# Feed-forward and MLP products: four high-weight products in a row, then four low-weight ones, in place of two and two

## Chip, cores and metric

The kernel runs on one core of a Trainium2 chip. The metric is the device time of one execution in microseconds (us). Before the change it is 2199.45 us, the median of three runs (2197.57 to 2200.47).

## What is computed

Two conditioned transformer stacks, one after the other, on 256 tokens of width 1024, all in float32. The first has two layers, each with a SwiGLU feed-forward of inner width 2816, a token mixer with two attention branches, and a second feed-forward. The second stack has a scan mixer, a window attention and three squared-ReLU MLPs of inner width 4096 (one of them for the context tokens). The change touches only the products of these two functions:

```python
def swiglu(x, w_gate, w_up, w_down):
    return (jax.nn.silu(x @ w_gate) * (x @ w_up)) @ w_down

def sq_relu_mlp(h, w1, w2):
    return jnp.square(jax.nn.relu(h @ w1)) @ w2
```

`swiglu` is called four times (stages F0, F1, F2, F3 of the kernel), `sq_relu_mlp` three times (Mc, M0, M1).

## The kernel before

**Float32 in three products.** A float32 matrix product is built from single-pass products of rounded operands (type fp32r). A weight w is split into a high part and a low part, w = hi + lo: ScalarE rounds a loaded chunk into `whi` (L1406), VectorE subtracts to get `wlo` (L1910). Activations are split the same way, and the two parts of one block of 128 features lie beside each other: 256 columns high, then 256 columns low. `xs` holds the split input of a stage (8 blocks), and `hs`, `hidden_arena`, `hidden_nraw` and `hidden_table` hold the split hidden values (22 blocks in a feed-forward, 32 in an MLP).

For one 128x128 block of weights TensorE issues two matmuls. `wide_hi` (L619) takes the high weights as the stationary operand and streams all 512 columns, high and low activations together, into one full bank of PSUM. `wide_lo` (L623) takes the low weights and streams the 256 high columns into the first half of the same bank. Each matmul has a weight load of its own, since no two neighbours use the same weights. In this document a "high step" or "hi" is a matmul of L619 and a "low step" or "lo" one of L623.

**Chunks.** Weights come from memory in chunks of 1 MB (2048 float32 in each of 128 partitions) through a ring of three: SyncE issues the load into `stage`, ScalarE writes `whi`, VectorE writes `wlo` and raises `lo_done`, TensorE uses the chunk and raises `chunk_used` with its last matmul, after which ScalarE may overwrite that `whi`. A chunk of the wide path is 16 weight blocks, so 16 hi and 16 lo.

**Order on TensorE.** It is written out by hand in the tensor block. `wide_first` (the first chunk of a stage) goes hi, hi, lo, lo over two output blocks of one input block, since its inputs arrive one by one. `wide_up` (all other chunks of the first products) takes one output block (`f`) at a time and goes through the eight input blocks `k` in pairs: hi of k and k+1, then lo of k and k+1. `wide_down` (second products) takes one of four output blocks (`d`) at a time and goes through the chunk's hidden blocks in pairs in the same way: four blocks in most chunks, two in the chunk of blocks 20 and 21 of a feed-forward, which is used twice. Every wait (for `lo_done`, for a drained bank, for hidden values) stands ahead of a chunk or between two `d`, never inside a pair. The mixers use another helper, `product` (L613, L614, L615), which issues three matmuls of 256 columns for each weight block, again with one weight load each; its order stays as it is. `keep_warm` (L688) issues matmuls of 512 bf16 columns ahead of some stages.

Of the kernel before, what the change touches and what calls it, by code (L numbers as in the profile page):

```python
# [95 lines left out]
class Signal:  # L96
# [15 lines left out]
    def at(self, key):  # L112
        if self.book["known"]:
            return self.book[self.name, key]
        return 1
# [3 lines left out]
def program(nc, A, out_ap, book):  # L119
    ctx = ExitStack()  # L120
    with ctx:
# [308 lines left out]
        def hidden(name, j):  # L430

            if j < 3:
                return hs[:, 2 * j:2 * j + 2, :, :]
            if name[0] == "F":
                at = (0, 4)[j - 3] if j < 5 else 16 + 4 * (j - 5)
                room = hidden_arena[:, at * 256:at * 256 + 1024]
            elif j < 5:
                room = hidden_nraw[:, (j - 3) * 1024:(j - 2) * 1024]
            elif j == 5:
                room = hidden_table[:]  # L440
            else:
                room = hidden_arena[:, (j - 6) * 1024:(j - 5) * 1024]
            return room.rearrange("p (f a t) -> p f a t", f=2, a=2)
# [154 lines left out]
        def _(pe):  # L598
# [18 lines left out]
            def wide_hi(out, w, pair, s, first_mm):  # L617

                return mm(out, whi[:, s, w:w + P], pair.rearrange("p a t -> p (a t)"), start=first_mm, stop=False, skip_group_check=True)  # L619

            def wide_lo(out, w, pair, s, last_mm):

                return mm(out[:, 0:T], wlo[:, s, w:w + P], pair[:, 0, :], start=False, stop=last_mm, skip_group_check=True)  # L623
# [34 lines left out]
            def wide_up(n, banks):  # L658

                pe.wait_ge(lo_done, START + n + 1)  # L660
                for f in range(2):
                    for k in range(0, 8, 2):
                        for kk in (k, k + 1):
                            wide_hi(banks[:, f, :], kk * 256 + f * P, xs[:, kk, :, :], n % RING, kk == 0)
                        for kk in (k, k + 1):
                            last = wide_lo(banks[:, f, :], kk * 256 + f * P, xs[:, kk, :, :], n % RING, kk == 7)
                last.then_inc(chunk_used, 1)

            def wide_down(n, name, blocks, d_at, banks, width, opens, closes, after=None):

                for d in range(4):
                    at = lambda i: i * width + (d_at + d) * P
                    pair = lambda i: hidden(name, blocks[i] // 2)[:, blocks[i] % 2, :, :]
                    for i in range(0, len(blocks), 2):
                        for ii in (i, i + 1):
                            wide_hi(banks[:, d, :], at(ii), pair(ii), n % RING, opens and ii == 0)
                        for ii in (i, i + 1):
                            last = wide_lo(banks[:, d, :], at(ii), pair(ii), n % RING, closes is not None and ii == len(blocks) - 1)
                    if closes and (d < 3 or width == 1024):
                        last.then_inc(pe_out.sem, pe_out.next(("y", name, closes, d)))  # L680
                    if after is not None:
                        after(d)
                return last
# [50 lines left out]
            def ffn(name):  # L734
                n = first[name]
                for j in range(PAIRS):
                    if j == 0:
                        wide_first(n, R[:, 0:2, :], name)
                    else:
                        pe.wait_ge(dve_out.sem, dve_out.at(("gate", name, j - 1)))  # L740
                        wide_up(n + 2 * j, R[:, 0:2, :])
                    turns(name, 2 * j)
                    if j:
                        pe.wait_ge(dve_out.sem, dve_out.at(("up", name, j - 1)))
                    wide_up(n + 2 * j + 1, R[:, 2:4, :])
                    turns(name, 2 * j + 1)
# [7 lines left out]
                for c in range(5):  # L754
                    pe.wait_ge(lo_done, START + n + c + 1)
                    if c == 0:
                        pe.wait_ge(dve_out.sem, dve_out.at(("gate", name, PAIRS - 1)))
                    pe.wait_ge(dve_out.sem, dve_out.at(("lo", name, 2 * c + 1)))
                    wide_down(n + c, name, range(4 * c, 4 * c + 4), 0, R, 512, c == 0, None, free if c == 0 else None) \
                        .then_inc(chunk_used, 1)  # L760
                    turns(name, 2 * PAIRS + c)
                pe.wait_ge(lo_done, START + n + 6)
                pe.wait_ge(dve_out.sem, dve_out.at(("lo", name, 10)))
                wide_down(n + 5, name, range(20, 22), 0, R, 1024, False, "R")
                pe.wait_ge(mod_taken, max(m for (at, w), m in turn_at.items() if at == name and w < 27) + 1)
                wide_down(n + 5, name, range(20, 22), 4, Y, 1024, True, None).then_inc(chunk_used, 1)
                turns(name, 27)

# [10 lines left out]
            def mlp(name):  # L779
                n = first[name]  # L780
                for j in range(UPS):
                    banks = R[:, 2 * (j % 2):2 * (j % 2) + 2, :]
                    if j == 0:
                        wide_first(n, banks, name)
                    else:
                        if j >= 2:
                            pe.wait_ge(dve_out.sem, dve_out.at(("up", name, j - 2)))
                        wide_up(n + j, banks)
                    turns(name, j)
# [1974 lines left out]
```

## Time and profile before

| | |
|---|---|
| median of 3 runs | 2199.45 us |
| profiled execution, its time | 2199.59 us |
| its span, first to last instruction | 2197.7 us |
| TensorE matmul busy | 2134.2 us, 97% |
| TensorE weight load busy | 1869.7 us, 85% |
| VectorE busy | 1799.1 us, 82% |
| ScalarE busy | 1184.3 us, 54% |
| DMA, mean of the span | 230 GB/s |
| mean granted TensorE clock | 0.992 |

The time lies 1.9 us above the span, for what precedes the first and follows the last instruction. Matmuls overlap in the records: a matmul of 512 columns is shown with about 0.39 us and its successor starts about 0.23 us after it. So for the pace of TensorE the distance from start to start counts and not the length of a record. In what follows a "step" is the time from the start of one matmul to the start of the next.

### The profile page before, as it was taken

To read this page: it belongs to the slowest core of one execution; us is meant where nothing else is said; L and a number is where in the kernel's file an instruction comes from. 1 tells how busy PE (TensorE), PEld (TensorE's weight loads), DVE (VectorE), ACT (ScalarE), POOL (GpSimd) and SP (SyncE) were. 2 spreads that over 40 slices of the span, in tenths; PEclk is the share of its full clock that TensorE was granted. 3 is DMA by queue.
4 is the path that set the end of the run, shared out by engine and by line. 5 is a ranking of instruction groups with operands and counts; after the bars stand their busy time and mean duration, and the time that the engine had idled before them with its cause. 6 is when DMAs were issued, how large, how long until landed. Compare 5 with 4: busy or idle time off the path is not lost.

```text
span 2197.7 us, 33877 instructions
## 1 busy us (share of the span) xinstructions
PE 2134.2 (97%) x14000; PEld 1869.7 (85%) x14000; DVE 1799.1 (82%) x2404; ACT 1184.3 (54%) x1785; POOL 109.5 (5%) x157
## 2 busy tenths in 40 slices
PE   7999999999999999999999999999999999999997
PEld 4888888888888889898889979888888888768886
DVE  4988787788878878877888787888998899788764
ACT  3555557455455445665544455447646744485742
POOL 1000000000000000000000000000000000000000
PEclk9999999999999999999999999999999999999999
DMA  9888666488858877655887727728878877405662
GB/s 332 287 285 315 222 221 209 135 269 286 306 197 278 290 251 258 205 183 189 278 288 254 270 92 234 249 78 291 287 284 271 296 257 258 134 5 167 214 211 77
DMA packets 330881, 506.28 MB, mean 230 GB/s; under 512 B 12375, under 2 KB 239926, under 8 KB 330727
## 3 DMA queue, kind: packets, MB, share of 16 engines
q1 hardware_dynamic: 288503, 341.75, 46.6%
q0 software_dynamic: 41616, 160.44, 20.8%
q8 instruction: 111, 1.82, 0.3%
q10 hardware_dynamic: 608, 1.92, 0.3%
q14 instruction: 43, 0.35, 0.0%
HBM read 503.03 MB, written 1.05 MB: 229 GB/s over the span
## 4 chain that ended last, share of the span: by engine, by line
PE 85%; DVE 9%; DMA 2%; ACT 2%; issue 1%; POOL 0%; DVEq 0%; POOLq 0%
PE banks L619 38%; PE banks L623 19%; PE banks L613 6%; PE banks L615 6%; PE banks L614 6%; DVE wlo L1910 1%; DMA plain_xs<-in_ada_w_dram 1%; PE banks L825 1%; PE banks L887 1%; DMA stage<-in_ffn_wg_dram 1%; DVE nraw L2188 1%; DVE arena L1935 1%; DVE xs L2192 1%; PE banks L720 1%; PE banks L721 1%
## 5 line engine op out<-in xcount | busy, mean ns | idle before, releaser
L1910 DVE TENSOR_TENSOR wlo<-stage,whi 128x1024 fp32r<-128x1024 f32 x644 | 758.2, 1219 | 131.2 <-ACT whi L1406 130.4
L1406 ACT CAST whi<-stage 128x1024 fp32r<-128x1024 f32 x644 | 643.7, 1051 | 335.4 <-PE banks L623 256.9
L619 PE MATMUL banks<-xs,whi 128*128 128x512 f32 x2176 | 687.4, 397 | 13.4 <-DVE xs L2192 9.5
L623 PEld LDWEIGHTS banks<-xs,wlo 128*128 128x128 f32 x2176 | 409.6, 188 | 96.9
L623 PE MATMUL banks<-xs,wlo 128*128 128x256 f32 x2176 | 428.2, 278 | 0.0
L613 PE MATMUL banks<-xs,whi 128*128 128x256 f32 x1216 | 351.8, 289 | 10.2 <-DVE xs L2192 4.8
L619 PEld LDWEIGHTS banks<-xs,whi 128*128 128x128 f32 x2176 | 331.6, 189 | 18.4 <-DVE xs L2192 7.6
L614 PE MATMUL banks<-xs,whi 128*128 128x256 f32 x1216 | 344.4, 283 | 0.0
L615 PE MATMUL banks<-xs,wlo 128*128 128x256 f32 x1216 | 344.4, 283 | 0.0
L619 PE MATMUL banks<-hidden_arena,whi 128*128 128x512 f32 x992 | 311.9, 395 | 0.0
L1935 DVE SCALAR_TENSOR_TENSOR arena<-modw,cact,arena 128x1024 f32<-128x1024 f32 x203 | 259.9, 1280 | 8.8 <-DMA modw<-in_w_mod_dram 4.3
L613 PEld LDWEIGHTS banks<-xs,whi 128*128 128x128 f32 x1216 | 233.5, 192 | 20.0 <-issue 9.0
L614 PEld LDWEIGHTS banks<-xs,whi 128*128 128x128 f32 x1216 | 233.8, 192 | 0.9 <-issue 0.5
L615 PEld LDWEIGHTS banks<-xs,wlo 128*128 128x128 f32 x1216 | 233.6, 192 | 0.0
L623 PEld LDWEIGHTS banks<-hidden_arena,wlo 128*128 128x128 f32 x992 | 186.5, 188 | 42.6
L623 PE MATMUL banks<-hidden_arena,wlo 128*128 128x256 f32 x992 | 195.8, 279 | 0.0
L619 PEld LDWEIGHTS banks<-hidden_arena,whi 128*128 128x128 f32 x992 | 150.1, 188 | 0.4
L594 POOL DMA_DIRECT2D modw<-in_w_mod_dram x80 | 57.1, 714 | 1142.5 <-DVE arena L1935 797.9
L619 PE MATMUL banks<-hs,whi 128*128 128x512 f32 x336 | 105.6, 395 | 0.0
L1426 ACT COPY hid<-banks 128x512 f32<-128x512 f32 x44 | 25.8, 587 | 112.8 <-PE banks L623 112.8
L594 POOL DMA_DIRECT2D modw<-in_ada_w_dram x64 | 45.7, 714 | 753.0 <-DVE arena L1935 668.7
L1422 ACT COPY hid<-banks 128x512 f32<-128x512 f32 x44 | 25.8, 587 | 105.2 <-PE banks L623 105.2
(413 smaller groups left out, 2692.9 us busy)
## 6 DMA issues: line engine op xcount, KB each, us to landing
stage<-in_mlp_w_dram SPq DMA_DIRECT2D x96, 1024.0 KB, 5.3
modw<-in_w_mod_dram POOLq DMA_DIRECT2D x80, 1024.0 KB, 5.9
modw<-in_ada_w_dram POOLq DMA_DIRECT2D x66, 1024.0 KB, 5.4
stage<-in_ffn_wg_dram SPq DMA_DIRECT2D x44, 1024.0 KB, 5.4
stage<-in_ffn_wu_dram SPq DMA_DIRECT2D x44, 1024.0 KB, 7.3
stage<-in_ffn_wd_dram SPq DMA_DIRECT2D x44, 1024.0 KB, 7.2
stage<-in_ev_w_in_dram SPq DMA_DIRECT2D x24, 1024.0 KB, 6.3
stage<-in_w_in_dram SPq DMA_DIRECT2D x18, 1024.0 KB, 5.2
```

What stands on the lines that cost most here:

```text
L594: pool.dma_start(modw[:, c % 2, :].rearrange("p (a b) -> p a b", a=2), src).then_inc(mod_landed[c % 2], 16)
L613: mm(out, hi, xh, start=first_mm, stop=False, skip_group_check=True)
L614: mm(out, hi, xl, start=False, stop=False, skip_group_check=True)
L615: return mm(out, lo, xh, start=False, stop=last_mm, skip_group_check=True)
L619: return mm(out, whi[:, s, w:w + P], pair.rearrange("p a t -> p (a t)"), start=first_mm, stop=False, skip_group_check=True)
L623: return mm(out[:, 0:T], wlo[:, s, w:w + P], pair[:, 0, :], start=False, stop=last_mm, skip_group_check=True)
L720: mm(out, xh, hi, start=k == 0, stop=False, skip_group_check=True)
L1406: nc.scalar.copy(halves(whi[:, s, :], n, h, True), halves(stage[:, s, :], n, h)).then_inc(hi_done, 1)
L1422: done(nc.scalar.copy(hid[:, j % 2, :, :], R[:, 0:2, T:2 * T]), ("gate", name, j))
L1426: done(nc.scalar.copy(hid[:, 2, :, :], R[:, 2:4, T:2 * T]), ("up", name, j - 1))
L1910: last = v.tensor_tensor(halves(wlo[:, s, :], n, h, True), halves(stage[:, s, :], n, h), halves(whi[:, s, :], n, h, True).bitcast(F32), AL ...
L1935: v.scalar_tensor_tensor(out=acc, in0=w, scalar=cc, in1=acc, op0=ALU.mult, op1=ALU.add).then_inc(mod_step, 1)
```

## The change

In `wide_up` and in `wide_down` the group that is taken first with the high and then with the low weights grows from two neighbouring blocks to four. `wide_first` stays. Where a chunk gives a group of only two blocks (blocks 20 and 21 of a feed-forward), the order stays as well. Which matmuls are issued, their number, operands, banks, waits and signals are the same.

```diff
@@ -659,10 +659,10 @@
 
                 pe.wait_ge(lo_done, START + n + 1)
                 for f in range(2):
-                    for k in range(0, 8, 2):
-                        for kk in (k, k + 1):
+                    for k in range(0, 8, 4):
+                        for kk in range(k, k + 4):
                             wide_hi(banks[:, f, :], kk * 256 + f * P, xs[:, kk, :, :], n % RING, kk == 0)
-                        for kk in (k, k + 1):
+                        for kk in range(k, k + 4):
                             last = wide_lo(banks[:, f, :], kk * 256 + f * P, xs[:, kk, :, :], n % RING, kk == 7)
                 last.then_inc(chunk_used, 1)
 
@@ -671,10 +671,11 @@
                 for d in range(4):
                     at = lambda i: i * width + (d_at + d) * P
                     pair = lambda i: hidden(name, blocks[i] // 2)[:, blocks[i] % 2, :, :]
-                    for i in range(0, len(blocks), 2):
-                        for ii in (i, i + 1):
+                    for i in range(0, len(blocks), 4):
+                        four = range(i, min(i + 4, len(blocks)))
+                        for ii in four:
                             wide_hi(banks[:, d, :], at(ii), pair(ii), n % RING, opens and ii == 0)
-                        for ii in (i, i + 1):
+                        for ii in four:
                             last = wide_lo(banks[:, d, :], at(ii), pair(ii), n % RING, closes is not None and ii == len(blocks) - 1)
```

TensorE in stage F0, at the end of one `wide_up` chunk, the eight transposes of a modulation vector (L825) and the start of the next chunk, before:

```order
L623 MATMUL banks<-xs,wlo 128x256 x2
L825 MATMUL banks<-base,arena 128x128 [waits mod_step]
L825 MATMUL banks<-base,arena 128x128 x7
L619 MATMUL banks<-xs,whi 128x512 [waits lo_done,dve_out]
L619 MATMUL banks<-xs,whi 128x512
L623 MATMUL banks<-xs,wlo 128x256 x2
L619 MATMUL banks<-xs,whi 128x512 x2
```

The same place with the change (L826 is L825 of before, one line further down):

```order
L623 MATMUL banks<-xs,wlo 128x256 x4
L826 MATMUL banks<-base,arena 128x128 [waits mod_step]
L826 MATMUL banks<-base,arena 128x128 x7
L619 MATMUL banks<-xs,whi 128x512 [waits lo_done,dve_out]
L619 MATMUL banks<-xs,whi 128x512 x3
L623 MATMUL banks<-xs,wlo 128x256 x4
```

The waits stand on the same matmul as before, the first hi of a chunk; behind it now follow three more hi and then four lo.

TensorE in stage F0, the last `wide_down` chunk, where the next stage's column sums (L831, L852) come in between two output blocks, before:

```order
L619 MATMUL banks<-hidden_arena,whi 128x512 x2
L623 MATMUL banks<-hidden_arena,wlo 128x256 x2
L831 MATMUL banks<-nraw,base 128x256 [waits dve_out]
L619 MATMUL banks<-hidden_arena,whi 128x512 x2
L623 MATMUL banks<-hidden_arena,wlo 128x256 x2
L619 MATMUL banks<-hidden_arena,whi 128x512 x2
L623 MATMUL banks<-hidden_arena,wlo 128x256 x2
L852 MATMUL banks<-nraw,base 128x256 [waits act_out]
```

And with the change (L832 and L853 are L831 and L852 of before):

```order
L619 MATMUL banks<-hidden_arena,whi 128x512 x4
L623 MATMUL banks<-hidden_arena,wlo 128x256 x4
L832 MATMUL banks<-nraw,base 128x256 [waits dve_out]
L619 MATMUL banks<-hidden_arena,whi 128x512 x4
L623 MATMUL banks<-hidden_arena,wlo 128x256 x4
L853 MATMUL banks<-nraw,base 128x256 [waits act_out]
```

What stands between two waits is the same set of matmuls in both; only inside it has the order changed.

## Rows read from the trace of the kernel before

**Rows 1.** The page: busy us (share of the span) xinstructions.

```profile
PE 2134.2 (97%) x14000; PEld 1869.7 (85%) x14000; DVE 1799.1 (82%) x2404; ACT 1184.3 (54%) x1785; POOL 109.5 (5%) x157
```

**Rows 2.** The page: the chain that ended last, by engine and by line.

```profile
PE 85%; DVE 9%; DMA 2%; ACT 2%; issue 1%; POOL 0%; DVEq 0%; POOLq 0%
PE banks L619 38%; PE banks L623 19%; PE banks L613 6%; PE banks L615 6%; PE banks L614 6%; DVE wlo L1910 1%; DMA plain_xs<-in_ada_w_dram 1%; PE banks L825 1%; PE banks L887 1%; DMA stage<-in_ffn_wg_dram 1%; DVE nraw L2188 1%; DVE arena L1935 1%; DVE xs L2192 1%; PE banks L720 1%; PE banks L721 1%
```

**Rows 3.** Busy time by stretch: window, length, busy per engine, clock, DMA share, GB/s.

```profile
core 0: us, PE busy (x) PEld busy (x) DVE busy (x) ACT busy (x) POOL busy (x), PEclk, DMA share, GB/s
100.00:142.00 42.00, 42.00 (x243) 36.67 (x243) 35.91 (x39) 22.05 (x30) 2.72 (x4) 1.00 0.85 280
185.00:222.00 37.00, 37.00 (x214) 32.41 (x213) 31.99 (x44) 18.03 (x21) 2.85 (x4) 1.00 0.95 338
```

**Rows 4.** Waits: who waited for whom, us in total, times, longest.

```profile
ACT whi L1406 <- PE banks L623: 256.9, 76, 5.0
...
PE banks L619 <- DVE xs L2192: 9.5, 15, 1.5
```

**Rows 5.** Line L619: number of hi by source of the activations, ns min/median/max.

```profile
L619 PE MATMUL banks<-xs,whi x2176: 387/396/633, 40.5 to 2094.5; 128*128 128x512 f32 x198
...
L619 PE MATMUL banks<-hidden_arena,whi x992: 388/398/587, 178.3 to 2184.3; 128*128 128x512 f32 x199
...
L619 PE MATMUL banks<-hs,whi x336: 390/395/475, 172.0 to 2149.4; 128*128 128x512 f32 x168
...
L619 PE MATMUL banks<-hidden_nraw,whi x96: 387/395/481, 1578.4 to 2155.0; 128*128 128x512 f32 x96
...
L619 PE MATMUL banks<-hidden_table,whi x48: 392/395/398, 1584.8 to 2155.7; 128*128 128x512 f32 x48
```

**Rows 6.** Timeline, PE, one `hidden_arena` stretch: start us, us; first and last pair of hi.

```profile
187.53 0.62 PE L619 MATMUL banks<-hidden_arena,whi 128*128 128x512 f32 x2
...
199.32 0.62 PE L619 MATMUL banks<-hidden_arena,whi 128*128 128x512 f32 x2
```

**Rows 7.** That stretch, L619 alone, busy time in its window; then ns min/median/max.

```profile
187.52:199.31 11.79, 10.61 (x34) 5.12 (x35) 1.00 0.96 344
...
L619 PE MATMUL banks<-hidden_arena,whi x34: 388/393/398, 187.5 to 198.8; 128*128 128x512 f32 x34
```

**Rows 8.** The same for L623.

```profile
187.95:199.70 11.75, 6.70 (x34) 6.36 (x34) 1.00 0.97 344
...
L623 PE MATMUL banks<-hidden_arena,wlo x34: 276/278/281, 188.0 to 199.2; 128*128 128x256 f32 x34
```

**Rows 9.** Timeline, PE, one `xs` stretch: first and last pair of hi.

```profile
99.37 0.63 PE L619 MATMUL banks<-xs,whi 128*128 128x512 f32 x2
...
141.17 0.63 PE L619 MATMUL banks<-xs,whi 128*128 128x512 f32 x2
```

**Rows 10.** That stretch: L619 alone, L623 alone; then groups, busy us and mean ns.

```profile
99.36:141.16 41.80, 37.69 (x120) 18.27 (x121) 1.00 0.86 285
...
99.82:141.60 41.78, 23.58 (x120) 22.54 (x120) 1.00 0.86 283
...
L619 PE MATMUL banks<-xs,whi 128*128 128x512 f32 x120 | 37.7, 395 | 0.0
...
L623 PE MATMUL banks<-xs,wlo 128*128 128x256 f32 x120 | 23.6, 278 | 0.0
```

**Rows 11.** Timeline of a mixer chunk of `product`: first and last matmul of 38 steps.

```profile
306.72 0.28 PE L613 MATMUL banks<-xs,whi 128*128 128x256 f32 x1
...
311.28 0.28 PE L615 MATMUL banks<-xs,wlo 128*128 128x256 f32 x1
```

**Rows 12.** Timeline: a `product` matmul and the weight load for its successor.

```profile
245.00 0.28 PE L615 MATMUL banks<-xs,wlo 128*128 128x256 f32 x1
245.00 0.19 PEld L613 LDWEIGHTS banks<-xs,whi 128*128 128x128 f32 x1
```

**Rows 13.** Timeline: twelve `keep_warm` matmuls in a row, ahead of stage F1.

```profile
427.30 2.78 PE L688 MATMUL banks<-base 128*128 128x512 bf16 x12
```

## Prediction

> **What bounds the kernel now.** I read the busy times first: matmuls fill 97% of the span, VectorE 82%, ScalarE 54% [rows 1]. A busy TensorE need not be a TensorE at its peak, so the chain comes next: 85% of the span hangs on PE, and 57% on the two lines that the change reorders, L619 and L623 [rows 2]. Then the stretches: in two clean ones of 42 and 37 us PE has no gap at all, at the full 2.4 GHz (clock 1.00), while VectorE is busy 35.91 of 42.00 us and ScalarE 22.05; DMA is busy 0.85 and 0.95 [rows 3]. Last the waits: ScalarE waits 256.9 us in total for L623 to free a chunk, TensorE's L619 only 9.5 us for its input [rows 4]. So in the wide products nobody but TensorE sets the pace, and what its order gains or loses there reaches the end one for one. A large gain would meet the DMA queues in the second products (0.95 [rows 3], 0.96 [rows 7]); a gain under 4% there would not.
>
> **What the change removes, adds and moves.** No matmul, load or wait is added or removed, so only the steps between neighbours count. First the number of places. There are 3648 hi (2176 + 992 + 336 + 96 + 48 [rows 5]) and as many lo. Of those, 112 of `xs` belong to the seven `wide_first` chunks (16 each) and 64 of `hidden_arena` to the chunks of blocks 20 and 21 (16 in each of four stages); both stay. The rest, 3472 hi, make 868 groups of four hi and four lo: 232 on `hidden_arena` ((992 - 64) / 4), 636 on other inputs.
>
> Before, such a group is two quads hi, hi, lo, lo, each with one step of the kinds HH, HL, LL and LH (from, to). After, it is hi x4, lo x4: three HH, one HL, three LL, one LH. Two HH and two LL of these eight stand where the trace has nothing: inside a longer run. Call those inner steps x (hi) and y (lo); the group changes by 2x + 2y minus one quad.
>
> The quads first. On `hidden_arena` 17 follow each other from 187.53 to 199.32 us: 693.5 ns each [rows 6]. On `xs` 60 from 99.37 to 141.17 us: 696.7 ns [rows 9]. HH and LL come out of the busy times, since two overlapping records cover one step plus the length of the second. `hidden_arena`: 10.61 us over 17 pairs is 624.1 ns, less the longer record of 398 ns, HH = 226.1 [rows 7]; 6.70 / 17 = 394.1, less 276, LL = 118.1 [rows 8] (that the second record is the longer of the hi and the shorter of the lo shows when single records are looked at). `xs`: 37.69 / 60 - 395 gives HH = 233.2, and 23.58 / 60 - 278 gives LL = 115.0 [rows 10]; here the mean length stands in for the second one's, good to 2 ns.
>
> My value: an inner step is as long as the step of its kind in a pair, x = HH and y = LL. It is the nearest row, the same matmuls with the same loads. Then a group on `hidden_arena` changes by 2 x (226.1 + 118.1) - 693.5 = -5.1 ns, one on `xs` by 2 x (233.2 + 115.0) - 696.7 = -0.3 ns; I give the other inputs, 120 of the 636 groups, the value of `xs`. The sum is 232 x -5.1 ns - 636 x 0.3 ns = -1.2 - 0.2 = **-1.4 us**.
>
> A second way to count says nearly the same. 1536 columns at 2.4 GHz are 640 ns, so a `hidden_arena` quad has 53.5 ns over, 13.4 for each matmul. In `product`, where all matmuls have 256 columns, 38 steps take 4.56 us [rows 11]: 120 ns, 13.3 over the 106.7 of the columns. So it looks as if every matmul with its own load costs some 13 ns on top, whatever its neighbours; then order costs and gives nothing, and HH 226 and LL 118 are those constants (226.7 and 120) with the starts of the records shifted by a few ns. That gives 0.0 us. Only the `xs` quads, at 14.2 a matmul, don't fit.
>
> The bounds of the unknown. For y: from 115 (LL on `xs`) to 120 [rows 11]. For x: below, twelve matmuls of 512 columns in bf16 cover 2.78 us [rows 13]; less one record of 0.39, that is 217 ns a step. Above, HL: HL and LH together are 349.3 and 348.5 ns (quad less HH and LL), less 115 for LH leaves 234. Low end x = 217, y = LL; high end x = 234, y = 120. One ns on x or on y costs 868 x 2 = 1.7 us.
>
> Cover: the hi and lo of a chunk are ready together, one wait for `lo_done`, and `chunk_used` comes with the last lo as before; SyncE, ScalarE and VectorE see the same events. If PE were a little faster, ScalarE's 256.9 us of waiting for it [rows 4] shows that the next chunk would be there. Banks are freed after the same last matmul.
>
> **The rivals.**
>
> *Slower: runs of lo are paced by their weight loads.* A load starts when the matmul before it starts and takes 0.19 us [rows 12]. Under a hi of 226 ns it is covered; under a lo it isn't, and the next matmul waits for its weights. In pairs only one lo follows a lo, and the time can be made good at the next hi; in `product` every matmul is short, and the steps are 120 ns [rows 11]. If inner lo steps are 120 while hi keep their 226 and 233, a group changes by 2 x 346.1 - 693.5 = -1.3 ns on `hidden_arena` and 2 x 353.2 - 696.7 = +9.7 ns elsewhere: -0.3 + 6.2 = +5.9 us, 2205.3. With x at its high end 234 too: 14.5 and 11.3 ns, +10.6 us, 2210. It decides from y about 2.5 ns above LL. Against it: where y is 120, the second count says that x falls too. The Trainium skill, "TensorE: Matmul & The Clock Gate", section "LDWEIGHTS (loading the stationary operand)", puts a load of P columns at P / 1.2 ns, an estimated 107 ns for 128, and "Back-to-back issue gap" a warm matmul of 256 columns at 109: by these the load would just fit under a lo and this rival had no ground. The 120 ns of [rows 11] speak against that.
>
> *Faster: hi in a run reach the pace of `keep_warm`.* If the excess of a hi is paid for the change of width beside it, inner hi run at 217. The groups change by 2 x (217 + 118.1) - 693.5 = -23.3 and 2 x (217 + 115.0) - 696.7 = -32.7 ns: -5.4 - 20.8 = -26.2 us, 2173. Halfway, x lies halfway between HH and 217: -14.1 and -16.5 ns, -13.8 us, 2185.7. For it: 217 has been seen for 512 columns. Against it: HH has no change of width between its two matmuls and is 226 to 233, and `product` has no change of width at all and pays 13 ns. The same section of the skill gives N / 2.4 + 2.5 for the step of a single kind, an estimated 216 and 109 ns; a quad of those is 650, so by it some 45 ns a quad would be the price of mixing, and halving the mixing would give more than this rival.
>
> *The change doesn't do what it says.* The order of instructions shows runs of four in both helpers, and two where there are two blocks. I give it nothing.
>
> **How the numbers follow.** The sum is made against the profiled execution, 2199.59 us (span 2197.7 and 1.9 around it), which is 0.14 above the median of the three runs; 2199.45 - 1.4 = **2198.0 us**. About 0.2% (4.4 us) is what a measurement of this kernel can tell from no change; that is 2.5 ns on x or y. Forecast, steps as in pairs: 0.60, its own range 2195.5 to 2201.5. Fixed price for each load, no change: 0.08. Loads pace the lo: 0.15. Hi speed up, wholly or in part: 0.17, of which 0.05 for the full size. So faster 0.17, same 0.68, slower 0.15. The range takes in the first two, most of the slower rival (to 2207) and the beginning of the faster one (from 2188), and leaves out about 0.18.
>
> **What the profile would show.** Right: `hidden_arena` and `xs` groups of eight take 1382 to 1394 ns, start of the first hi to the start of the next group's, with inner hi at 0.23 and inner lo at 0.115 to 0.12, and the busy sums of L619 and L623 as now. Slower rival: inner lo at 0.12 on `xs`, hi unchanged. Faster rival: inner hi under 0.225. Wrong in another way: a gap ahead of a first hi that wasn't there, or new waits on `lo_done`; then the pace isn't TensorE's own, as I took it to be.

## The result and the profile after

The changed kernel takes 2205.72 us, the median of 7 runs (2202.13 to 2209.91), against 2199.61 us for the kernel before in 7 runs (2197.57 to 2201.73). The ratio is 1.0026, with a 95% interval of 1.0017 to 1.0036: slower by a quarter of a per cent, a little over what can be told from no change. The profiled execution took 2203.93 us with a span of 2202.1.

The page of the changed kernel: busy times, and the chain by line.

```profile
PE 2137.5 (97%) x13991; PEld 1873.8 (85%) x14000; DVE 1798.6 (82%) x2404; ACT 1184.8 (54%) x1785; POOL 109.5 (5%) x157
...
PE 86%; DVE 9%; DMA 2%; ACT 2%; issue 1%; ACTq 0%; DVEq 0%
PE banks L619 38%; PE banks L623 19%; PE banks L613 6%; PE banks L615 6%; PE banks L614 6%; DVE wlo L1911 1%; PE banks L888 1%; PE banks L826 1%; DVE nraw L2189 1%; PE banks L910 1%; DMA stage<-in_ffn_wg_dram 1%; DVE xs L2193 1%; DVE arena L1936 1%; DMA modw<-in_ada_w_dram 1%; PE banks L721 1%
```

Against [rows 1, 2] the other engines are as they were, and TensorE has 3 us more (nine matmul records are missing in this trace, of 14000). Its waits in the wide products are the same too (who waited for whom, us, times, longest; compare [rows 4]):

```profile
ACT whi L1407 <- PE banks L623: 254.6, 75, 5.3
...
PE banks L619 <- DVE xs L2193: 9.5, 15, 1.5
```

So the time is in the steps. TensorE's timeline on `xs` (start us, us), two groups in a row and the last of a stretch of 29:

```profile
98.97 1.09 PE L619 MATMUL banks<-xs,whi 128*128 128x512 f32 x4
99.90 0.63 PE L623 MATMUL banks<-xs,wlo 128*128 128x256 f32 x4
100.37 1.09 PE L619 MATMUL banks<-xs,whi 128*128 128x512 f32 x4
...
139.66 1.09 PE L619 MATMUL banks<-xs,whi 128*128 128x512 f32 x4
```

40.69 us over 29 groups are 1403.1 ns a group. Before, two quads took 2 x 696.7 = 1393.4 [rows 9]. That is +9.7 ns. And the same on `hidden_arena`:

```profile
184.81 1.09 PE L619 MATMUL banks<-hidden_arena,whi 128*128 128x512 f32 x4
...
197.29 1.09 PE L619 MATMUL banks<-hidden_arena,whi 128*128 128x512 f32 x4
```

12.48 us over 9 groups are 1386.7 ns, against 2 x 693.5 = 1387.0 [rows 6]: nothing. Which steps grew on `xs` shows in the busy time of L623 alone, first on `xs`, then on `hidden_arena` (window, length, PE busy; below each the shortest, median and longest record):

```profile
99.89:140.11 40.22, 18.45 (x116) 17.61 (x115) 1.00 0.85 273
...
L623 PE MATMUL banks<-xs,wlo x116: 278/280/283, 99.9 to 139.5; 128*128 128x256 f32 x116
```

```profile
185.73:197.70 11.97, 5.59 (x36) 5.29 (x35) 1.00 0.97 341
...
L623 PE MATMUL banks<-hidden_arena,wlo x36: 276/276/281, 185.7 to 197.2; 128*128 128x256 f32 x36
```

A run of four overlapping records covers three steps and the last record. On `xs` 18.45 / 29 = 636.2, less 280, is 356.2 for three steps: LL = 118.7, where pairs had 115.0 [rows 10]. On `hidden_arena` 5.59 / 9 = 621.1, less 276, gives LL = 115.0, where pairs had 118.1 [rows 8]. The same instructions with the same loads go up in one place and down in the other. 516 groups on `xs` at +9.7 ns are +5.0 us, and 232 on `hidden_arena` nothing.

### The profile page after: what moved, and what is told of

Read it like the earlier page. It is cut to its first block, busy times and chain, and to the rows that moved or that the text cites. A ratio compares the mean times of both kernels' runs of the same rounds, so it can differ in the third digit from the quotient of the medians.

```text
span 2202.1 us, 33868 instructions
## 1 busy us (share of the span) xinstructions
PE 2137.5 (97%) x13991; PEld 1873.8 (85%) x14000; DVE 1798.6 (82%) x2404; ACT 1184.8 (54%) x1785; POOL 109.5 (5%) x157
## 4 chain that ended last, share of the span: by engine, by line
PE 86%; DVE 9%; DMA 2%; ACT 2%; issue 1%; ACTq 0%; DVEq 0%
PE banks L619 38%; PE banks L623 19%; PE banks L613 6%; PE banks L615 6%; PE banks L614 6%; DVE wlo L1911 1%; PE banks L888 1%; PE banks L826 1%; DVE nraw L2189 1%; PE banks L910 1%; DMA stage<-in_ffn_wg_dram 1%; DVE xs L2193 1%; DVE arena L1936 1%; DMA modw<-in_ada_w_dram 1%; PE banks L721 1%
## 5 line engine op out<-in xcount | busy, mean ns | idle before, releaser
L619 PE MATMUL banks<-xs,whi 128*128 128x512 f32 x2176 | 601.4, 396 | 12.2 <-DVE xs L2193 9.5
L619 PEld LDWEIGHTS banks<-xs,whi 128*128 128x128 f32 x2176 | 369.5, 189 | 64.6 <-DVE xs L2193 7.6
L623 PEld LDWEIGHTS banks<-xs,wlo 128*128 128x128 f32 x2176 | 337.6, 189 | 49.0
L613 PE MATMUL banks<-xs,whi 128*128 128x256 f32 x1216 | 351.1, 289 | 10.9 <-DVE xs L2193 5.6
L623 PE MATMUL banks<-xs,wlo 128*128 128x256 f32 x2176 | 350.3, 281 | 0.0
L615 PE MATMUL banks<-xs,wlo 128*128 128x256 f32 x1216 | 343.9, 283 | 0.0
L614 PE MATMUL banks<-xs,whi 128*128 128x256 f32 x1216 | 343.9, 283 | 0.0
L619 PE MATMUL banks<-hidden_arena,whi 128*128 128x512 f32 x992 | 277.8, 396 | 0.0
L613 PEld LDWEIGHTS banks<-xs,whi 128*128 128x128 f32 x1216 | 232.9, 192 | 20.8 <-issue 9.1
L614 PEld LDWEIGHTS banks<-xs,whi 128*128 128x128 f32 x1216 | 233.0, 192 | 0.9 <-issue 0.5
L615 PEld LDWEIGHTS banks<-xs,wlo 128*128 128x128 f32 x1216 | 233.0, 192 | 0.0
L619 PEld LDWEIGHTS banks<-hidden_arena,whi 128*128 128x128 f32 x992 | 168.5, 188 | 21.8
L623 PEld LDWEIGHTS banks<-hidden_arena,wlo 128*128 128x128 f32 x992 | 153.3, 188 | 22.3
L623 PE MATMUL banks<-hidden_arena,wlo 128*128 128x256 f32 x992 | 159.8, 278 | 0.0
L619 PE MATMUL banks<-hs,whi 128*128 128x512 f32 x336 | 96.4, 395 | 0.2 <-issue 0.2
```

Source lines behind the costliest of these rows:

```text
L613: mm(out, hi, xh, start=first_mm, stop=False, skip_group_check=True)
L614: mm(out, hi, xl, start=False, stop=False, skip_group_check=True)
L615: return mm(out, lo, xh, start=False, stop=last_mm, skip_group_check=True)
```

## Experiments

All times are medians, and ratios are to the kernel before, run on the same chip, with 95% intervals.

| kernel | us | ratio | interval |
|---|---|---|---|
| fours in `wide_up` only | 2204.42 | 1.0024 | 1.0015 to 1.0033 |
| fours in `wide_down` only | 2200.16 | 0.9999 | 0.9990 to 1.0008 |
| eights in `wide_up` | 2200.32 | 0.9999 | 0.9990 to 1.0008 |
| ones in both | 2207.11 | 1.0033 | 1.0020 to 1.0045 |
| fours, 64 bytes ahead of `xs` | 2190.70 | 0.9956 | 0.9944 to 0.9969 |
| pairs, 64 bytes ahead of `xs` | 2189.39 | 0.9950 | 0.9937 to 0.9964 |
| fours, 64 bytes ahead of `whi` | 2205.69 | 1.0025 | 1.0016 to 1.0034 |
| fours, 128 bytes ahead of `xs` | 2201.71 | 1.0005 | 0.9996 to 1.0013 |
| fours, 64 bytes ahead of `wlo` | 2195.12 | 0.9974 | 0.9965 to 0.9982 |
| pairs, 64 ahead of `xs` and of the arena | 2185.64 | 0.9925 | 0.9912 to 0.9938 |
| fours, the same layout | 2187.30 | 0.9941 | 0.9929 to 0.9953 |
| eights in `wide_up`, the same layout | 2181.93 | 0.9920 | 0.9907 to 0.9933 |

### One part of the change at a time

Runs of four in `wide_up` alone:

```diff
-                    for k in range(0, 8, 2):
-                        for kk in (k, k + 1):
+                    for k in range(0, 8, 4):
+                        for kk in range(k, k + 4):
```

> Runs of four in wide_up only (516 of the 868 groups, all on xs); wide_down stays in pairs. In the trace of the change a group of four hi and four lo takes 1402.8 ns on xs against 2 x 696.7 before (+9.4), and 1387.3 on hidden_arena against 2 x 694.0 (none). Theory A (the price is on inputs placed like xs, hs and hidden_nraw, whose inner lo steps are 119 ns): 516 x 9.4 ns = +4.9 us against before, most of what the change costs. Theory B (the price comes from a place other than the steps, such as a wait or a chunk boundary in wide_down): +2 us or less here.

Measured: 2204.42 against 2199.99 us, +4.4. Then the same in `wide_down` alone:

```diff
-                    for i in range(0, len(blocks), 2):
-                        for ii in (i, i + 1):
+                    for i in range(0, len(blocks), 4):
+                        for ii in range(i, min(i + 4, len(blocks))):
```

> Runs of four in wide_down only; wide_up stays in pairs. Theory A: 232 groups on hidden_arena at no price, some 84 on hs at +5 ns and 36 on hidden_nraw and hidden_table at +5 to +13 ns: +0.4 to +1 us in all, no difference that can be measured. Theory B (the price is not in the steps of the xs groups): +3 us or more here.

Measured: 2200.16, +0.2. Within their intervals the two parts add up to the whole (1.0024 and 0.9999 against 1.0026), and the part on `xs` has nearly all of it. Theory A stands as to the place; it says nothing yet of the reason.

### Other lengths of run

Eight hi and then eight lo in `wide_up`, pairs in `wide_down`:

```diff
-                    for k in range(0, 8, 2):
-                        for kk in (k, k + 1):
+                    for k in range(0, 8, 8):
+                        for kk in range(k, k + 8):
```

> Runs of eight hi and eight lo in wide_up, wide_down in pairs. Price per inner step (a hi or lo with its like on both sides): fours have 4 inner hi and 4 inner lo per sixteen matmuls of xs and cost 18.8 ns, eights have 6 and 6. Theory A, a price for each inner step: 28 ns on a group of sixteen, 2787 to 2815, times 258 = +7.3 us against before. A price for the four-run alone (a pattern of the order that eights don't have): less than the +4.9 of up_only. Rival, the excess belongs to the change of width: eights have half the changes of fours and get faster than they, under +4.9.

Measured: 2200.32, +0.3 and not +7.3, so a price for each inner step is wrong. TensorE's timeline, first and last of 14 groups of sixteen, and the busy time of L623 in that stretch:

```profile
98.90 2.00 PE L619 MATMUL banks<-xs,whi 128*128 128x512 f32 x8
100.74 1.11 PE L623 MATMUL banks<-xs,wlo 128*128 128x256 f32 x8
...
138.00 2.00 PE L619 MATMUL banks<-xs,whi 128*128 128x512 f32 x8
```

```profile
100.73:139.83 39.10, 15.62 (x112) 15.28 (x112) 1.00 0.84 277
...
L623 PE MATMUL banks<-xs,wlo x112: 277/283/283, 100.7 to 137.9; 128*128 128x256 f32 x112
```

39.10 / 14 = 2792.9 ns for sixteen matmuls: 14.6 ns a matmul over the columns (eight times 768 columns at 2.4 GHz are 2560 ns). Pairs have 14.2 and fours 15.4. Seven LL cover 15.62 / 14 - 283 = 832.7 ns, 119.0 each. Read one by one in the trace, the lo steps of such a run are 113, 119, 120, 120, 120, 120, 120 and the hi steps 233, 236, 228, 232, 231, 227, 227, 227. The lo have settled after two steps and the hi after five, both on 13.3 ns over their columns. A change of kind is followed by some uneven steps. They aren't the same in every order: three lo steps in a row on `xs` are 117.5, 119.7 and 118.6 in fours, and 113, 119 and 120 at the start of eights, so a run of four isn't a run of eight cut short.

Runs of one:

```diff
-                    for k in range(0, 8, 2):
-                        for kk in (k, k + 1):
+                    for k in range(0, 8, 1):
+                        for kk in range(k, k + 1):
...
-                    for i in range(0, len(blocks), 2):
-                        for ii in (i, i + 1):
+                    for i in range(0, len(blocks), 1):
+                        for ii in range(i, min(i + 1, len(blocks))):
```

> Runs of one: hi, lo, hi, lo in wide_up and wide_down alike (wide_first stays). There are no steps from hi to hi or from lo to lo. If length of a run is what costs on xs (weight loads that lag behind in a run of lo), ones are no slower than pairs: 693 to 697 ns per four matmuls, 0 to -4 us against before. If pairs were already the best length (changing width costs too), ones are slower: over 700 ns per four matmuls, +3 us or more. hidden_arena, where every length has cost 13.3 ns a matmul so far: 693 to 694 either way.

Measured: 2207.11, +7.1. TensorE's timeline on `xs` and on `hidden_arena`:

```profile
117.94 0.40 PE L619 MATMUL banks<-xs,whi 128*128 128x512 f32 x1
...
119.33 0.40 PE L619 MATMUL banks<-xs,whi 128*128 128x512 f32 x1
```

```profile
189.88 0.40 PE L619 MATMUL banks<-hidden_arena,whi 128*128 128x512 f32 x1
...
191.29 0.40 PE L619 MATMUL banks<-hidden_arena,whi 128*128 128x512 f32 x1
```

Four hi and four lo lie between the rows of each: 1.39 us on `xs`, about as in pairs, but 1.41 on `hidden_arena`, where pairs take 1387 ns; read from the starts of single matmuls over all its stages, the mean there is 353.2 ns for one hi and one lo, 1413 for four of each. 232 times 26 ns are 6.0 of the 7.1 us. So the slow place has moved: alternation costs on `hidden_arena` and not on `xs`, fours the other way round. I had expected every length to be free on `hidden_arena`, and that was wrong. Neither the length of a run nor the load behind a lo explains a price that changes sides; the two inputs must differ in something else. It could be where they lie in memory, or what the other engines and the DMA do in the stages that read them; the next kernels tell these apart.

### The place of the operands

```diff
+        pad = sb("pad", [P, 16])
         xs = sb("xs", [P, KB, 2, T], F32R)
```

> The changed kernel with 64 unused bytes per partition laid ahead of xs: xs, hs, hid, hidden_nraw, hidden_table and the arena all move up by 64, stage, whi and wlo stay. Before the move the starts of whi, wlo, xs, hs and nraw are 0 and the arena's is 64 in bytes modulo 128; after it xs, hs and nraw are at 64 and the arena at 0. Theory C (what a group costs over 13.3 ns a matmul depends on where the streamed operand lies against the weights): the roles are swapped, groups of eight on xs and hs take 1387 instead of 1401 to 1403, on hidden_arena 1400 or more instead of 1387; 516 + 84 groups gain 15 ns, 232 lose 15: 2206 - 9 + 3.5, some 2200 us. Theory D (the place within 128 bytes is nothing; the stage or the distance in memory decides): all groups as in the changed kernel, 2205 to 2206 us.

> The kernel before, in pairs, with the same 64 unused bytes ahead of xs. Theory C: quads on xs, hs and hidden_nraw 693.3 instead of 696.7 to 698, on hidden_arena 697 instead of 694: 1250 quads gain 3.5 to 4 ns, 480 lose 3, -3 us, 2197. Theory D: 2200, quads as before.

Measured: 2190.70 in fours, 2189.39 in pairs, both far faster than before. TensorE's timeline in fours (L620 is the hi line here), on `xs` and on `hidden_arena`:

```profile
99.37 1.07 PE L620 MATMUL banks<-xs,whi 128*128 128x512 f32 x4
...
140.87 1.07 PE L620 MATMUL banks<-xs,whi 128*128 128x512 f32 x4
```

```profile
185.58 1.09 PE L620 MATMUL banks<-hidden_arena,whi 128*128 128x512 f32 x4
...
198.20 1.09 PE L620 MATMUL banks<-hidden_arena,whi 128*128 128x512 f32 x4
```

41.50 / 30 = 1383.3 ns on `xs`, 12.62 / 9 = 1402.2 on `hidden_arena`. The roles are swapped: `hidden_arena`, moved to distance 0, takes what `xs` took there. The gain was sized too small, because `xs` at 64 is below the 1387 I took and because `product` gains as well. Added up from the starts of all matmuls in the two profiled executions of pairs (10.7 us apart), the wide products on `xs` give 8.3 us and lose 1.8 on `hidden_arena`; `product` on `xs` gives 4.4, though some 3500 of its steps are 2.2 ns shorter, which would be 7.8. The rest went into longer waits in the mixers, where TensorE isn't alone in setting the pace. The timeline of `product` in the kernel of pairs (L614 and L616 are L613 and L615 of before):

```profile
302.48 0.28 PE L614 MATMUL banks<-xs,whi 128*128 128x256 f32 x1
...
306.96 0.28 PE L616 MATMUL banks<-xs,wlo 128*128 128x256 f32 x1
```

38 steps in 4.48 us, 117.9 ns instead of 120 [rows 11].

Is it the distance or the place itself? The same 64 bytes ahead of `whi` move weights and operands together:

```diff
+        pad = sb("pad", [P, 16])
         whi = sb("whi", [P, RING, CH], F32R)
```

> The changed kernel with the 64 unused bytes ahead of whi: whi, wlo and all that follows move up together, so weights and streamed operands keep their distance and only the absolute place changes. If the distance between the two counts: as the changed kernel, xs groups 1403 and hidden_arena groups 1387, 2205 to 2206 us. If the absolute place of the streamed operand counts: as with the pad ahead of xs. Theory D: as the changed kernel.

Measured: 2205.69, the time of the changed kernel. And with 128 bytes ahead of `xs` (32 columns in place of 16):

> The changed kernel with 128 unused bytes ahead of xs: xs from 128 to 0 and the arena from 64 to 192 in bytes modulo 256. If only the place modulo 128 counts (theory C in its narrow form): as the changed kernel, 1403 on xs and 1387 on hidden_arena, 2205 to 2206 us. If the place counts on a wider scale: the groups on xs or on hidden_arena change.

Measured: 2201.71. The timelines of both, on `xs`:

```profile
98.89 1.09 PE L620 MATMUL banks<-xs,whi 128*128 128x512 f32 x4
...
139.59 1.09 PE L620 MATMUL banks<-xs,whi 128*128 128x512 f32 x4
```

```profile
99.69 1.10 PE L620 MATMUL banks<-xs,whi 128*128 128x512 f32 x4
...
141.83 1.10 PE L620 MATMUL banks<-xs,whi 128*128 128x512 f32 x4
```

The first, moved with the weights, has 40.70 / 29 = 1403.4 ns, as without a pad. The second, at distance 128, has 42.14 / 30 = 1404.7. On `hidden_arena`, which the 128 bytes bring to distance 64:

```profile
187.03 1.09 PE L620 MATMUL banks<-hidden_arena,whi 128*128 128x512 f32 x4
...
199.48 1.07 PE L620 MATMUL banks<-hidden_arena,whi 128*128 128x512 f32 x4
```

12.45 / 9 = 1383.3, what `xs` has at 64. The narrow form of theory C is therefore wrong, 128 bytes do make a difference; modulo 256 the groups on `xs` and `hidden_arena` so far fit one row each of this table, whichever of the two they read:

| distance | four hi and four lo, ns | seen on |
|---|---|---|
| 0 | 1403.1, 1403.4, 1402.2 | `xs`, `xs`, `hidden_arena` |
| 64 | 1383.3, 1383.3 | `xs`, `hidden_arena` |
| 128 | 1404.7 | `xs` |
| 192 | 1386.7 | `hidden_arena` |

Two rivals are out. The absolute place isn't the cause, and neither is the distance to `stage`, since the pad ahead of `whi` changed both and the time stayed (2205.69 us); the work of the stages isn't either, since the roles of the two inputs swapped while the stages stayed. The period of 256 is less certain. The weight blocks start at multiples of 512 bytes, and modulo 512 the four rows are 0, 64, 128 and 448, which fits as well. Nor is the distance all. At 128 the groups on `xs` repeat 1396, 1411 and 1406 ns in turns of three, though a chunk has four of them, so the length of a group also depends on what came before it; 1404.7 is the mean over thirty.

How long a group takes thus hangs on the streamed operand and the weights together. The Trainium skill, "TensorE: Matmul & The Clock Gate", section "Step-by-step: what each phase is for", says that the next weights are loaded over a read port of their own and take nothing from the running matmul. These groups don't bear that out: with all instructions the same, 64 bytes between the operands are worth 20 ns in 1403. By what path one disturbs the other no run here shows.

### Which of the two weights

The pad between `whi` and `wlo` gives each its own distance:

```diff
+        pad = sb("pad", [P, 16])
         wlo = sb("wlo", [P, RING, CH], F32R)
```

> The changed kernel with the 64 unused bytes between whi and wlo: xs is at distance 64 from whi and 0 from wlo; hidden_arena at 0 from whi and 192 from wlo. Theory C in its sharp form (a step's length hangs on the stream and on the weights that are loaded meanwhile, whi in the steps to a hi, wlo in the steps to a lo): on xs the steps hi to hi are those of distance 64 (229.6, 232.4, 230.4) and the steps lo to lo those of distance 0 (119.5, 118.8, 118.4), a group about 1390 to 1396. If one of the two weights alone decides: 1383 (whi) or 1403 (wlo).

Measured: 2195.12. TensorE's timeline on `xs`, and L624 (the lo line) alone in that stretch:

```profile
100.87 1.08 PE L620 MATMUL banks<-xs,whi 128*128 128x512 f32 x4
...
142.48 1.08 PE L620 MATMUL banks<-xs,whi 128*128 128x512 f32 x4
```

```profile
101.78:143.39 41.61, 19.06 (x120) 18.34 (x120) 1.00 0.85 277
...
L624 PE MATMUL banks<-xs,wlo x120: 277/283/283, 101.8 to 142.4; 128*128 128x256 f32 x120
```

A group takes 41.61 / 30 = 1387.0 ns; three LL take 19.06 / 30 - 283 = 352.3, 117.4 each, between distances 0 (118.7) and 64 (115.5 in the trace with the pad ahead of `xs`). On `xs` that leans towards the sharp form: most of the gain is in the hi, whose weights are at 64. But the steps aren't those it named (the hi are 226, 229 and 232, the lo 113, 119 and 120), and the group lies below its 1390 to 1396. And `hidden_arena`, with `whi` at 0 and `wlo` at 192, speaks against it:

```profile
186.86:200.12 13.26, 6.37 (x40) 5.94 (x39) 1.00 0.97 341
...
L624 PE MATMUL banks<-hidden_arena,wlo x40: 280/281/283, 186.9 to 199.8; 128*128 128x256 f32 x40
```

The last record of a run is the longest here, so three LL cover 6.37 / 10 - 283 = 354 ns, 118.0 each. With `wlo` still at 192 the sharp form wants the 115.0 of before the pad. So a step isn't set by its own stream and the weights loaded meanwhile alone. Both distances count, and how they act together is open.

### The order again, in a better layout

64 bytes ahead of `xs` and 64 more ahead of the arena put `xs`, `hs` and `hidden_arena` all at distance 64:

```diff
+        pad = sb("pad", [P, 16])
         xs = sb("xs", [P, KB, 2, T], F32R)
...
+        pad2 = sb("pad2", [P, 16])
         arena = sb("arena", [P, 47 * 256])
```

> The order of before (pairs), 64 unused bytes ahead of xs and 64 more ahead of the arena. Distance from the weights to the streamed operand modulo 256, so far: xs 0 before, 64 with the first pad; hidden_arena 192 before, 0 with the first pad, 64 here. At 64 the groups of four on hidden_arena took 1382.9 ns, at 192 1387, at 0 1402.6. If the distance is all: quads on hidden_arena 690 to 693 instead of 696.8 with one pad, 480 of them, so 2 to 3 us off the 2189.4 of one pad: 2187. If the arena's other users (DVE and ScalarE tiles) mind the place: no gain or a loss.

> The order of the change (fours) in the same layout. At distance 64 a group on xs takes 1383.4 ns in fours and 2 x 690.3 in pairs, +2.8; on hidden_arena 1382.9 against 2 x 690 to 693. If the price of fours hangs on distance 0, it shrinks from +16 ns (against 13.3 a matmul) to nothing here and the whole difference to pairs_both is 636 x 2.8 ns = +1.8 us at most, 2189. If fours cost something of their own in any place: +4 to +6 us as before.

> Runs of eight in wide_up and pairs in wide_down, in the same layout. If the pace inside a long run is a fixed 13.3 ns over the columns wherever the operand lies (as the last steps of eights were, 226.7 and 120.0): 2773 ns for sixteen, against 2761 in pairs at this distance, +3 us. If the pace depends on the distance all along: product chains at distance 64 took 117.4 a step instead of 119.9, so a group of sixteen takes 2740 to 2765 and the kernel 2185 to 2188.

Measured: pairs 2185.64, fours 2187.30, eights 2181.93. The timelines on `xs` of pairs (62 quads), fours (30 groups) and eights (14 groups of sixteen):

```profile
99.64 0.62 PE L621 MATMUL banks<-xs,whi 128*128 128x512 f32 x2
...
142.41 0.62 PE L621 MATMUL banks<-xs,whi 128*128 128x512 f32 x2
```

```profile
100.86 1.09 PE L621 MATMUL banks<-xs,whi 128*128 128x512 f32 x4
...
142.36 1.09 PE L621 MATMUL banks<-xs,whi 128*128 128x512 f32 x4
```

```profile
100.59 2.00 PE L621 MATMUL banks<-xs,whi 128*128 128x512 f32 x8
...
139.18 2.00 PE L621 MATMUL banks<-xs,whi 128*128 128x512 f32 x8
```

Brought to sixteen matmuls these are 4 x 689.8 = 2759, 2 x 1383.3 = 2767 and 2756 ns. At distance 0 they were 2787 [rows 9], 2806 and 2793. The penalty of fours against pairs falls from 19 ns to 7, that of the whole kernel from 6.1 us to 1.7, and the intervals of the two ratios overlap. Of eights I had expected 2773 if a long run settles on a fixed 13.3 ns over the columns, and 2740 to 2765 if it doesn't. Both occur. Two neighbouring runs of lo:

```profile
102.42 1.07 PE L625 MATMUL banks<-xs,wlo 128*128 128x256 f32 x8
...
105.16 1.11 PE L625 MATMUL banks<-xs,wlo 128*128 128x256 f32 x8
```

Read start by start, groups of 2741 ns, whose lo steps are all 113.3, take turns with groups of 2772, whose first lo step is 120 and the others 117.8 in the mean. A chunk has one group for each of two output blocks, but which of the two is the fast one changes in the course of the trace. So the operands' place doesn't fix it either: a group seems to inherit something from the one before it, and what that is stays open. The fastest kernel of this study, by its median, is the one with eights in `wide_up`, pairs in `wide_down` and the two pads: 0.9920 of before (0.9907 to 0.9933). Whether its order beats pairs in the same layout (0.9925) these runs don't tell; the steps give it 3 ns in 2759, under 1 us.

## Why the prediction was wrong

**What bounds the kernel** was read rightly. TensorE has no gap in the clean stretches, no wait changed, and the steps account for the difference: 516 x 9.7 ns = 5.0 us on `xs`, and the part with `wide_up` alone gives +4.4 of the +6.1 between the medians. Between the two profiled executions the difference is 4.3 us.

**The count** of 868 groups, 232 of them on `hidden_arena`, held, and so did the cover: the other engines' busy times and TensorE's waits in the wide products stayed as they were.

**The step that failed is the value for y, the inner lo step.** I set it to LL of a pair, 115.0 ns on `xs`, as the nearest row. Four lo in a row have a mean LL of 118.7 there. The hi didn't pay for it: the group grew by 9.7 ns. Read start by start in the 29 groups, the three LL are 355.8 ns where the forecast had 345.0, the three HH 700.7 against 699.6, and HL and LH together 346.8 against 348.5; so y is the term that was mis-sized on `xs`, and x was right there. On `hidden_arena` the same rule, an inner step as long as its kind in a pair, promised a gain of 5.1 ns, and there was 0.3, since x and y missed in opposite senses: three HH are 692.7 against 678.3, three LL 345.0 against 354.3. There the second count, a fixed 13.3 ns for each matmul, was the better one. That count also carried the warning. It fitted `hidden_arena` and the `product` chain, and the `xs` quads had 0.9 ns a matmul too much. I noted the misfit and went on, when 636 of the 868 groups lay on the side that didn't fit.

**The slower rival** came close to the result, +5.9 us and 2205.3, with +9.7 ns on inputs other than `hidden_arena` and about none on it, and I gave it 0.15. Its mechanism is only half right. Longer runs of lo did slow down on `xs`. But a load alone doesn't pace them: at another distance lo run at 115.5 with the same loads, on `hidden_arena` at 115.0, and eights at distance 0 cost next to nothing against pairs (2793 against 2787 ns) although their lo stand at 120. What the runs show to count is how load and stream lie to each other, together with the order.

**The faster rival** is out. No inner hi came near 217 ns; the shortest steps between two hi are 224. That changing between 512 and 256 columns has a price, as its rule has it, is borne out by one case, ones on `hidden_arena`, with 13 ns in 706, and refuted by eights, which with half the changes of fours and a quarter of those of pairs are not faster than pairs at distance 0.

**The range** (2188 to 2207) held the time, by its upper part, which was there for the slower rival. That is no merit of the forecast itself: its own range ended at 2201.5, and its sign was wrong.

**Still open.** Why the sum of the uneven steps after a change of kind is largest for runs of four at distance 0, how the distances to `whi` and to `wlo` act together, whether the period is 256 bytes or 512, and what one group hands on to the next. No run here looked inside a step.

## What to carry to other kernels

Where TensorE is gapless, an edit that only reorders matmuls can still move the time by a few ns a step, and the sign can't be read off steps that stand in another order: measure the new order on one stage, or leave both signs open. When a simple count fits some inputs and misses others by one ns a matmul, find out what sets them apart before trusting either side. And look at where the operands lie: here 64 unused bytes ahead of a buffer brought nearly twice what the new order had cost.

## What the runs showed of the hardware

- The pace of single-pass float32 matmuls with a weight load each depends on the distance in bytes between weights and streamed operand in the partition, here counted modulo 256 (modulo 512 fits as well): 1403 ns for four matmuls of 512 and four of 256 columns at 0, 1383 at 64, 1405 at 128, 1387 at 192. Moving both together changed nothing (2205.69 against 2205.72 us).
- The `product` chain, three matmuls of 256 columns for each weight block, goes from 120 to 117.9 ns a step with the distance from 0 to 64.
- In long runs at distance 0 both kinds settle on 13.3 ns over their columns, 226.7 and 120.0 ns, the lo after two steps and the hi after five.
- The same instructions at the same distance can still take two or three lengths in turn: eights at distance 64 take 2741 and 2772 ns, fours at distance 128 take 1396, 1411 and 1406.
- The same edit of 64 bytes took 10.9 us off the kernel before (0.9950, 0.9937 to 0.9964), and a second one brought it to 0.9925.
